# Spreading the position-bias table later: a GpSimd stretch and its 2.6 MB transfer moved from the first block to the second

## The reference: what is computed

```python
def rel_bucket(rel):
    nb = REL_BUCKETS // 2          # 16
    max_exact = nb // 2            # 8
    ret = jnp.where(rel > 0, nb, 0)
    n = jnp.abs(rel)
    ...
    return ret + jnp.where(n < max_exact, n, large)

# in dsa_mixer, per block of 128 queries
score = jnp.einsum('bqhs,bqh->bqs', jax.nn.relu(s_idx), wb)        # index scores
top_val, top_idx = lax.top_k(score, n_sel)                          # 128 keys a query
logits = jnp.einsum('bqhc,bqkc->bhqk', q_lat, c_sel) * ATT_HEAD_DIM ** -0.5
bias = rel_bias[rel_bucket(top_idx - qpos[None, :, None])]          # (32, 8) table
logits = logits + jnp.moveaxis(bias, -1, 1)
```

## Time and profile before

| | us |
|---|---|
| median of 3 runs (2194.65 to 2196.27) | 2196.22 |
| time of the profiled execution | 2196.22 |
| its span | 2194.4 |
| TensorE busy | 2087.9 (95%) |
| VectorE busy | 1061.4 (48%) |
| ScalarE busy | 749.7 (34%) |
| GpSimd busy | 229.7 (10%) |
| load of a weight unit, issue to landing (median of 155) | 4.8 |
| write of the bias table, issue to landing | 56.0 |

### The profile page before, as it was taken

The page is one execution under the profiler, slowest core; times in us unless marked ns, Lnnn a source line. Parts: engine busy times, 40 slices in busy tenths (PEclk is TensorE's granted clock), DMA queues, the critical chain, the costliest instruction groups (busy, mean ns, idle before and its releaser), DMA issues.

```text
span 2194.4 us, 28790 instructions
## 1 busy us (share of the span) xinstructions
PE 2087.9 (95%) x11578; PEld 1763.2 (80%) x11578; DVE 1061.4 (48%) x1429; ACT 749.7 (34%) x975; POOL 229.7 (10%) x198
## 2 busy tenths in 40 slices
PE   7998988999999999999899999999998899999997
PEld 5776656768888888898899999999886578888885
DVE  5654547454444454313244343435598634443434
ACT  4435653353223243331332222123434433222122
POOL 2001022020000022002320000002035210000001
PEclk9997789999999999899899999999999899999998
DMA  4213112212222222111122222222222022222221
GB/s 165 81 74 48 21 39 77 96 58 96 96 96 93 90 86 97 55 61 39 39 90 84 96 94 79 96 96 96 77 77 72 7 77 96 96 96 96 96 84 69
DMA packets 27792, 174.68 MB, mean 80 GB/s; under 512 B 4385, under 2 KB 4513, under 8 KB 7730
## 3 DMA queue, kind: packets, MB, share of 16 engines
q1 hardware_dynamic: 25680, 167.32, 21.5%
q0 software_dynamic: 1856, 5.90, 1.7%
q10 hardware_dynamic: 162, 0.10, 0.0%
HBM read 168.53 MB, written 4.78 MB: 79 GB/s over the span
## 4 chain that ended last, share of the span: by engine, by line
PE 69%; issue 18%; DVE 7%; ACT 4%; POOL 1%; DMA 0%; DVEq 0%; POOLq 0%; ACTq 0%
PE lin L425 56%; PE aux L1959 1%; ACT w_hi L359 1%; PE lin L1140 1%; DVE w_lo L366 1%; PE lin L1150 1%; PE aux L1528 1%; PE aux L1542 1%; POOL squares L601 1%; PE lin L1929 1%; PE aux L1943 1%; PE aux L1119 1%; PE aux L1120 1%; PE aux L1955 0%; PE aux L1556 0%
## 5 line engine op out<-in xcount | busy, mean ns | idle before, releaser
L425 PE MATMUL lin<-v_hi,w_hi 128*128 128x264 f32 (+1 forms) x1712 | 573.7, 335 | 4.8 <-DVE v_lo L586 3.4
L425 PE MATMUL lin<-v_hi,w_lo 128*128 128x264 f32 (+1 forms) x1712 | 571.1, 334 | 0.0
L425 PE MATMUL lin<-v_lo,w_hi 128*128 128x264 f32 (+1 forms) x1712 | 569.5, 333 | 0.0
L425 PE MATMUL lin<-x_hi,w_hi 128*128 128x512 f32 (+1 forms) x1224 | 436.2, 356 | 29.2 <-DMA cst<-in_consts 13.4
L425 PE MATMUL lin<-x_hi,w_lo 128*128 128x512 f32 (+1 forms) x1224 | 433.0, 354 | 0.0
L425 PE MATMUL lin<-x_lo,w_hi 128*128 128x512 f32 (+1 forms) x1224 | 432.6, 353 | 0.0
L366 DVE TENSOR_TENSOR w_lo<-w_raw,w_hi 128x2048 fp32r<-128x2048 f32 (+1 forms) x144 | 328.7, 2282 | 195.9 <-ACT w_hi L359 195.8
L359 ACT ACTIVATE w_hi<-w_raw 128x2048 fp32r<-128x2048 f32 (+1 forms) x155 | 292.9, 1890 | 289.9 <-PE lin L425 285.4
L425 PEld LDWEIGHTS lin<-v_hi,w_hi 128*128 128x128 f32 x1712 | 324.5, 190 | 39.6 <-DVE v_lo L586 3.8
L425 PEld LDWEIGHTS lin<-v_lo,w_hi 128*128 128x128 f32 x1712 | 324.4, 189 | 33.7 <-issue 0.7
L425 PEld LDWEIGHTS lin<-v_hi,w_lo 128*128 128x128 f32 x1712 | 324.3, 189 | 32.1
(11 more groups left out here) (341 smaller groups left out, 2358.9 us busy)
## 6 DMA issues: line engine op xcount, KB each, us to landing
w_raw<-in_weights SPq DMA_DIRECT2D x155, 1024.0 KB, 4.8
rel_by_distance<-rel_vec POOLq DMA_DIRECT2D x1, 2620.0 KB, 56.0
rel_bias<-rel_by_distance POOLq DMA_DIRECT2D x8, 264.0 KB, 3.0
h<-in_x_t SPq DMA_DIRECT2D x4, 512.0 KB, 8.2
out_t<-h SPq DMA_DIRECT2D x4, 512.0 KB, 2.8
mem_in<-in_mem_t POOLq DMA_DIRECT2D x1, 1024.0 KB, 5.1
cst<-in_consts SPq DMA_DIRECT2D x1, 512.0 KB, 9.8
col<-in_cols ACTq DMA_DIRECT2D x1, 67.0 KB, 6.0
```

Of the source, the lines that this page charges most:

```text
L425: last = nc.tensor.matmul(o, a, b, start=(k % (L.kc // k_banks) == 0 and p == 0), stop=((k + 1) % (L.kc // k_banks) == 0 and p == 2))
```

## The change

The load of `rel_row`, the 31 copies and the DMA that writes the table are taken from GpSimd's program in the first block, and put behind the squares of the last layer's norm (`l_mix1`), ahead of `next_splits_after(pool, C_)`. The wait for `y_gated` goes, since `rel_vec` gets another place in memory, in the region `before_x`, ahead of the index keys; these (`ki_t`, `ki_hi`, `ki_lo`, `qi_parts`) lie 655 floats further on. The old place becomes part of a filler.

```diff
@@ build: memory
         wi_tok = sb("wi_tok", [P, 4, 8], scope=before_x)
+        rel_vec = sb("rel_vec", [8, T2 + P - 1], scope=before_x)
         ki_t = sb("ki_t", [P, T2], scope=before_x)
@@
         sb_k_2 = sb("sb_k_2", [P, 2, S1], F32R, scope=phase)
-        rel_vec = sb("rel_vec", [8, T2 + P - 1], scope=phase)
-        sb("rest_of_zs", [P, 2 * S1 - 656], scope=phase)
+        sb("rest_of_zs", [P, 2 * S1], scope=phase)
@@
-        def pool_distance_bias(pool):
-
-            pool.wait_ge(sem("y_gated"), 4)
-            pool.wait_ge(sem("rel_loaded"), 16)
-            for s, e, b in bucket_runs()[0]:
-                ins = nc.gpsimd.tensor_copy(rel_vec[:, s:e], rel_row[:, b:b + 1].broadcast_to([8, e - s]))
-            ins.then_inc(sem("rel_spread"), 1)
-            pool.wait_ge(sem("rel_spread"), 1)
-            pool.dma_start(rel_dram, rel_vec[:, :].unsqueeze(1).broadcast_to([8, P, VEC]))\
-                .then_inc(sem("rel_kept"), 16)
@@ GpSimd's program
-            pool.dma_start(rel_row[:, :], rel_t).then_inc(sem("rel_loaded"), 16)
             pool_squares(pool, l_mix, 0)
-            pool_distance_bias(pool)
             pool_squares(pool, l_ssd, l_ssd.idx)
...
             for N in (l_ffn0, l_mix1):
                 pool_squares(pool, N, N.idx)
 
+            pool.dma_start(rel_row[:, :], rel_t).then_inc(sem("rel_loaded"), 16)
+            pool.wait_ge(sem("rel_loaded"), 16)
+            for s, e, b in bucket_runs()[0]:
+                ins = nc.gpsimd.tensor_copy(rel_vec[:, s:e], rel_row[:, b:b + 1].broadcast_to([8, e - s]))
+            ins.then_inc(sem("rel_spread"), 1)
+            pool.wait_ge(sem("rel_spread"), 1)
+            pool.dma_start(rel_dram, rel_vec[:, :].unsqueeze(1).broadcast_to([8, P, VEC]))\
+                .then_inc(sem("rel_kept"), 16)
             next_splits_after(pool, C_)
             dve_splits(pool, C_, nc.gpsimd)
```

## The result

| | kernel before | changed kernel |
|---|---|---|
| median, us (lowest to highest) | 2195.43 (2187.81 to 2196.27), 4 runs | 2210.22 (2204.78 to 2216.03), 4 runs |
| ratio to before, 95% interval | 1 | 1.0064 [1.0045, 1.0085] |
| profiled execution: time, span | 2196.22, 2194.4 | 2211.32, 2209.5 |

The change makes the kernel slower by 14 us, between 10 and 19 by the interval. (The medians of four alone would give 1.0067; the record of the result lists 18 runs of the changed kernel, 2201.01 to 2216.03 us.) The forecast was 2196.2 us, no change, with a range up to 2199.5.

What follows compares the result with a forecast made beforehand. TensorE was taken to bound the kernel (69% of the chain, GpSimd 1%, DMA 0%). Five terms of 0 each left the profiled 2196.22 us at a forecast of 2196.2 us, no change, range 2192 to 2199.5.

Steps and rivals of the forecast that it cites:

- Step 4: New place, table transfer against three weight loads: AQ's unit 0 lands 1.5 us later, still 11.8 us early; cost 0.
- the three bounds of the step: Unit 0's load beside the table: loses nothing, 6.6 us by fair turns, or 14.0 us, landing 0.6 us late.
- The nearest row: At 1663 to 1671 a weight load overlapping two `rel_bias` loads took 5.7 instead of 4.8 us; scaled to 1.5 us.
- Rival A: Engines don't switch queues during the table's transfer, so unit 0's split starts 37.6 us late: 2233.8 us; 4%.
- Rival B: Slower by other contention, longer weight load or blocked VectorE copies: up to 10 us more, 2201 to 2206 us; 4%.
- Step 5: GpSimd's first `w_lo` against VectorE's L1832 near 1574: a shifted wait could give -3.9 to +0.6 us; taken as 0.
- Step 1: Old place, 7.69 us of GpSimd work removed between idle times: 0 to -0.5 us; taken as 0.
- Step 2: New place on GpSimd: small load, copies and DMA issue hidden by 24 us of slack; cost 0.
- Step 3: New place on VectorE: RECIPROCAL and L2106 beside the copies, at most 0.1 us; taken as 0.
- C: Faster: old place gives back 0.5 us and the L1832 lock 3.9 us, 2191.8 us; 4%.
- The signs named for a wrong forecast: ScalarE waiting for a load near 1572, or the stage before 310 us shorter by more than 0.5 us.

Runs made afterwards that it cites:

- the transfer behind unit 0: The changed kernel with the table's DMA issued after GpSimd's wait for unit 1's landing; 2190.17 us, ratio 0.9986.
- the second transfer: The kernel before, its own table untouched, with another DMA of the table's shape added at the new place; 2202.35 us, ratio 1.0046.

## Why the prediction was wrong

**Step 4 failed, in how it sized contention.** It read "46.1% of the 16 engines" as each engine busy for 46% of the time, and set 32 of the table's packets on each of 16. It is 64 packets on each of 8 engines, back to back, and none on the others; 512 x 0.82 us / 8 = 52 us is the transfer's whole length. The row itself had the hint: the transfer took 56.0 us though half of the engines' time was free, and a transfer that is alone has no reason to leave gaps. Two views could have shown it, the packets' time against the landing time as just done, and the diff's own shape, a source of 8 partitions. With 8 full engines none of the three bounds of the step holds: not "the load slips into the idle 54%" (that time is on the wrong engines), not 6.6 us, not even the 14.0 us taken as the far end, which gave a load of 18.8. Measured: 24.8, of which 16.0 us passed before the held half moved at all.

**The nearest row misled.** At 1663 to 1671 a load and `rel_bias` cost each other 0.9 us. But q0 had 16.7% there and never kept an engine busy. It shows that two queues can share; it says nothing of a queue whose packets stand waiting on the engine. I scaled it by 46.1/16.7, as though the price were linear in the share.

**Rival A had the mechanism in part, and got 4%.** It said that an engine doesn't turn to the load while it has the table's packets. That is what 7 us without one q1 packet show. It went wrong in the size: it held the load until the transfer's end (a wait of 37.6 us), and the engines let it through 16 us after its issue, 31 us before the transfer's end. The Trainium skill, DMA: Bandwidth & Descriptors, section "SWDGE vs HWDGE vs iDMA", says that an engine switches only at packet boundaries and takes its queues in turn. The second half of the load does alternate 1:1 with the table once it moves; the wait ahead of that isn't explained by turns among the profile's packets of 0.82 us, and no run shows whether one of those is what the page calls a packet. What sets it was not found (below).

**Rival B** (contention of another sort, up to 10 us, 2201 to 2206, also 4%) stood in the right place, ScalarE waiting for a load past 1572. It named no mechanism, and the measured 2210.22 lies above its end.

**Step 5: right in the small, and too narrow.** "Late unit 1 frees L1832 and blocks one of L1835" came out so: 4285 ns before, then 4035 on L1835. But it looked at one meeting of VectorE and GpSimd only. GpSimd's row of `w_lo` goes on through AQ, and VectorE's norm lies in it; L758 was 0.87 us clear of a `w_lo` in the kernel before. This term, 4.0 us in the changed kernel, stood nowhere in the sum. It was readable from the profile before: L758 had a margin of 0.87 us, and whatever shifts VectorE against GpSimd by some tenths can spend it. Not all of VectorE's work is exposed: the rounds of the top-k search run beside a `w_lo` at their usual length (L1857 0.69 us at 1647.09, inside the one that starts at 1646.86).

**A third term, 2.0 us,** was missed too: a stall on TensorE can cost more than its length when the granted clock falls behind it (0.50 from 1581 to 1589). How much of the 2.0 is clock and how much the moved lock isn't separated.

**What was right.** Step 1: nothing came back at the old place (0.29 against 0.27 us a wait). Step 2: copies at 1540 to 1545, hidden, and stage 166.89 with them alone. Step 3: the same run. C fell with that: no gain from L1832, neither in the changed kernel nor where `w_lo` of unit 0 was VectorE's. The signs named for a wrong forecast were the ones that came: ScalarE waiting for a load near 1574.

**What stays open.** What lets the held half through. Where no held load stood ahead of it and the transfer was a single one that went on, it was nearly the same time from the issue to the first packet on the held engines: 16.0 us in the changed kernel, 15.9 in its second profile, 15.7 with the transfer behind unit 0, 15.1 for the third load beside the second transfer. For the third load beside ScalarE's transfer it was 15.3, with packets of half the size. So it is neither a count of the table's packets nor the place in the transfer. The half-size transfer fits too (23.7 us to landing). Behind eight DMAs in a row it was over 20. What sets the 15 to 16 us no run shows, and no kernel here varies packet size alone. Also open is why two kernels with a longer stage aren't slower.

## What to carry to other kernels

A share of DMA time is a mean over 16 engines: ask on how many of them a transfer lies before its neighbour's slack is computed, and test with its own length (packets x us per packet / landing time is the number of engines, here 7.5). A transfer from few partitions that runs for tens of us belongs where no load is awaited, or on 128 partitions, where the same bytes took 15.4 us and cost nothing. Cutting it into several DMAs made it worse. And when one engine of a pair that blocks each other is shifted, go through the whole row of meetings, not only the first one.

## What was unexpected of the hardware

- A 1 MB load issued during a 2.6 MB transfer on 8 engines took 24.8, 24.3, 23.6 and 21.5 us instead of 4.8, half of it moving at once and half only 15 to 16 us after the issue (where no held load stood ahead); behind 8 smaller DMAs in a row 35.0.
- It is much the same from ScalarE's queue (21.4, 20.9) as from GpSimd's.
- One source shape of 8 partitions moved 2620 KB in 56 to 59 us, 47 GB/s; of 128 partitions in 15.4 us, 174 GB/s. Spread over all 16 engines by eight DMAs, the 8 partitions gave no more (0.40 MB in 8 us).
- After 5 of 7 us without work TensorE was granted 0.50 for 8 us, in which it was busy for 6.
- A VectorE instruction that starts some tenths of a us behind GpSimd's `w_lo` waits for nearly all of its 4.6 us; one that had already begun costs GpSimd 0.5.
